# Second expert stage of a two-block model: sixteen weight slots on the chip, the expert sum kept in the residual, the silu written in place

## The reference, cut to what matters

```python
x  = ln_affine(ALPHA * x + (1 + m[2]) * hyena(h), ln_g[0], ln_b[0])
hl = modulate(x, m[3], m[4])
# 16 experts; each one takes the 64 tokens with the highest affinity for it:
#   y[tokens] += affinity * ((silu(hl[tokens] @ w1) * (hl[tokens] @ w3)) @ w2)
x  = ln_affine(ALPHA * x + (1 + m[5]) * y, ln_g[1], ln_b[1])
```

## Time and profile before

| | us |
|---|---|
| median of 3 runs | 2311.09 |
| lowest, highest | 2307.94, 2311.12 |
| the profiled execution's own time | 2322.09 |
| its span, first to last instruction | 2320.1 |

### The profile page before, as it was taken

The page is one execution under the profiler, slowest core; times in us unless marked ns, Lnnn a source line. Parts: engine busy times, 40 slices in busy tenths (PEclk is TensorE's granted clock), DMA queues, the critical chain, the costliest instruction groups (busy, mean ns, idle before and its releaser), DMA issues.

```text
span 2320.1 us, 25225 instructions
## 1 busy us (share of the span) xinstructions
PE 1948.7 (84%) x9836; PEld 1138.1 (49%) x9836; DVE 755.2 (33%) x1283; ACT 539.6 (23%) x910; POOL 273.7 (12%) x187
## 2 busy tenths in 40 slices
PE   7888978785898983899988599888888888888886
PEld 5776876563454552687976233232333333333332
DVE  5546333333332325565873601011010101010103
ACT  4765544321212124431133300000000000000002
POOL 1750700002222222000420000000000000000000
PEclk9897989897999996899998699999999999999998
DMA  5641461037999955122223189999999999999993
GB/s 195 236 181 67 188 260 62 0 154 268 391 402 419 402 222 219 73 91 91 73 73 138 81 350 413 422 413 421 413 422 414 421 414 422 414 421 415 420 416 151
DMA packets 127896, 640.87 MB, mean 276 GB/s; under 512 B 13675, under 2 KB 30443, under 8 KB 72908
## 3 DMA queue, kind: packets, MB, share of 16 engines
q1 hardware_dynamic: 112956, 606.78, 65.0%
q0 software_dynamic: 4304, 16.52, 1.9%
q10 hardware_dynamic: 10560, 16.52, 1.9%
HBM read 608.83 MB, written 30.93 MB: 276 GB/s over the span
## 4 chain that ended last, share of the span: by engine, by line
PE 46%; DMA 30%; DVE 9%; ACT 6%; POOL 6%; issue 2%; SPq 1%; ACTq 0%; DVEq 0%; POOLq 0%
PE psum L818 45%; DMA ring<-in_w 28%; DVE arena L1843 2%; POOL arena L779 2%; PE psum L816 2%; ACT arena L1502 1%; DVE weights_low L1843 1%; ACT arena L1475 1%; DVE arena_low L1843 1%; DVE arena L1851 1%; POOL arena L775 1%; DMA ring<-in_stream 1%; POOL arena L776 1%; ACT arena L1509 1%; DVE arena L1847 1%
## 5 line engine op out<-in xcount | busy, mean ns | idle before, releaser
L818 PE MATMUL psum<-ring,arena 128*64 128x512 f32 x3816 | 855.6, 596 | 122.4 <-DMA ring<-in_w 111.7
L818 PEld LDWEIGHTS psum<-ring,arena 128*64 128x64 f32 x3816 | 297.7, 137 | 653.0 <-issue 636.9
L1475 ACT ACTIVATE arena<-psum 128x512 f32<-128x512 f32 (+3 forms) x231 | 119.8, 544 | 1051.7 <-PE psum L818 992.4
L1843 DVE TENSOR_TENSOR arena<-psum,arena 128x512 f32<-128x512 f32 (+1 forms) x112 | 73.2, 653 | 662.4 <-PE psum L818 555.2
L818 PE MATMUL psum<-arena_low,weights_high 128*128 128x512 f32 (+1 forms) x704 | 255.6, 382 | 7.1 <-DVE weights_low L1843 7.1
L818 PE MATMUL psum<-features_high_part,weights_high 128*128 128x512 f32 x576 | 232.8, 404 | 33.5 <-DVE weights_low L1843 15.1
L818 PE MATMUL psum<-features_high_part,weights_low 128*128 128x512 f32 x576 | 229.6, 399 | 0.0
L818 PE MATMUL psum<-arena 128*128 128x512 f32 (+4 forms) x514 | 189.2, 525 | 11.4 <-ACT arena L1475 9.7
L1843 DVE TENSOR_TENSOR weights_low<-ring,weights_high 128x2048 fp32r<-128x2048 f32 x46 | 110.2, 2400 | 153.4 <-ACT weights_high L1493 144.9
L816 PE MATMUL psum<-ident,arena 128*128 128x128 f32 (+2 forms) x556 | 79.9, 290 | 87.4 <-DVE arena L1847 31.9
L818 PEld LDWEIGHTS psum<-arena_low,weights_high 128*128 128x128 f32 x704 | 134.0, 197 | 30.7 <-DVE weights_low L1843 7.3
(11 more groups left out here) (241 smaller groups left out, 1639.3 us busy)
## 6 DMA issues: line engine op xcount, KB each, us to landing
ring<-in_w SPq DMA_DIRECT2D x384, 1024.0 KB, 20.2
ring<-in_moe SPq DMA_DIRECT2D x93, 1024.0 KB, 10.3
ring<-in_stream SPq DMA_DIRECT2D x54, 1024.0 KB, 6.8
arena<-in_stream SPq DMA_DIRECT2D x16, 1024.0 KB, 4.9
in_spectra<-ring ACTq DMA_DIRECT2D x8, 1024.0 KB, 23.9
ring<-in_spectra SPq DMA_DIRECT2D x8, 1024.0 KB, 5.9
x_places<-scratch POOLq DMA_DIRECT2D x1, 7936.0 KB, 36.8
arena<-x_places SPq DMA_DIRECT2D x15, 512.0 KB, 12.0
```

What stands on the lines that cost most here:

```text
L818: ins_ = pe.matmul(o, lhs, rhs, start=start, stop=stop)
L1475: bk.emptied.inc(act.activation(dst, o, func, **more))
L1843: return dve.tensor_tensor(dst, a, b, op)
```

## The change

- The stage has 16 slots. Twelve are the ring as before. Four lie in the arena: two in region 1 (where `y2` was), one in the upper half of region 2, one in the upper half of region 3 (where `silu2` was). Slot 12 is loaded only after the last output of the second layer normalisation, since region 1 is read until then.
- `y2` and its memset are gone. Each scatter product is multiplied by (1 + m[5]) and added to `x`, which has been multiplied by ALPHA before the loop. The eight steps behind the loop are gone, and the last layer normalisation reads `x`; PE's first means wait for DVE's emptying of the scatter banks instead of `s_res`.
- The silu is written into `hid2`, and DVE multiplies in place.
- `y_sel`, `onehot`, `onehot_g` move to region 4, `scat` to `scratch`.

```diff
--- before.py
+++ after.py
@@ -34,7 +34,8 @@
 COLS = UNIT // KD
 RING = 5
 RING1 = 9
-RING2 = 12
+RING2 = 16
+WHOLE = 12
 ALPHA = 2.0 ** 0.25
 LN_EPS = 1e-5
 MOD_EPS = 1e-6
@@ -249,7 +250,7 @@
 
 
 
-        ring = under("ring", [P, RING2, UNIT])
+        ring = under("ring", [P, WHOLE, UNIT])
         w_low = [part(f"weights_low{r}", [P, UNIT]) for r in range(RING + 1)]
         w_high = [part(f"weights_high{r}", [P, UNIT]) for r in range(HIGH)]
         f_high = part("features_high_part", [P, KD, S])
@@ -400,15 +401,16 @@
         window_const = nc.inline_tensor(filter_windows(), "filter_windows").ap()
 
         h_tok = region(5, 0, ST, D)
-        y2 = region(1)
         x_sel = region(2, 0, 1, D)
         x_sel_t = region(2, 1024, KD, P)
-        y_sel = region(2, 2048, 1, D)
-        onehot = region(2, 3072, ST, P)
-        onehot_g = region(2, 3584, ST, P)
-        hid2, silu2 = region(3, 0, 1, FF), region(3, 2048, 1, FF)
+        y_sel = region(4, 2048, 1, D)
+        onehot = region(4, 3072, ST, P)
+        onehot_g = region(4, 3584, ST, P)
+        hid2 = region(3, 0, 1, FF)
         hid2_t = region(4, 0, FF // P, P)
-        scat = arena[:, 4, 2048:2560]
+        scat = scratch[:, 0, :]
+        moe2_slot = [ring[:, n, :] for n in range(WHOLE)] + [arena[:, 1, UNIT * b:UNIT * b + UNIT] for b in range(2)]
+        moe2_slot += [arena[:, 2, UNIT:2 * UNIT], arena[:, 3, UNIT:2 * UNIT]]
         aff_t = arena[0:NE, 4, 2560:3072]
         work_t = arena[0:NE, 4, 3072:3584]
         mask_t = arena[0:NE, 4, 3584:4096]
@@ -542,7 +544,7 @@
                 slot_ = turn[0] % slots
                 if used.i is not None or turn[0] >= slots:
                     sp.wait_ge(s_used, used.at(1 - slots))
-                dst = ring[:, slot_, :]
+                dst = moe2_slot[slot_] if arrived is s_arrived2 else ring[:, slot_, :]
                 if dst_shape is not None:
                     dst = dst_shape(dst)
                 sp.dma_start(dst, src).then_inc(arrived[slot_], 16)
@@ -699,6 +701,8 @@
                 for name in ("w1", "w3"):
                     for k in range(KD):
                         for e in range(2):
+                            if name == "w1" and 2 * k + e == WHOLE:
+                                sp.wait_ge(s_lno, 6 * KD)
                             load(ins[name][2 * i + e, k])
                 for k in range(KD):
                     for e in range(2):
@@ -835,7 +839,7 @@
                 pe.wait_ge(arrived[slot_], v)
                 turn[0] += 1
                 unit_no.n += 1
-                return ring[:, slot_, :]
+                return moe2_slot[slot_] if arrived is s_arrived2 else ring[:, slot_, :]
 
             def used():
                 owed.append(s_used)
@@ -1453,7 +1457,7 @@
                     mm(o, y_sel[:, 0, P * n:P * n + P], scat, True, True, bk_d)
                 assert not owed
                 leave(entry)
-            layer_norm(region(2), region(3), lambda k: pe.wait_ge(s_res, KD + k + 1))
+            layer_norm(x, region(3), summed)
 
 
         @block.scalar
@@ -1795,7 +1799,7 @@
                 bk.filled.enter(i, 12)
                 bk.emptied.enter(i, 12)
                 for n in range(4):
-                    empty(take(), silu2[:, 0, 512 * n:512 * n + 512], ACT.Silu)
+                    empty(take(), hid2[:, 0, 512 * n:512 * n + 512], ACT.Silu)
                 gathered()
                 for n in range(2):
                     o = take()
@@ -2473,8 +2477,6 @@
                     ins_.then_inc(s_aff, 1)
                 else:
                     do(ins_)
-            dve.wait_ge(s_lno, 6 * KD)
-            do(dve.memset(y2, 0.0))
 
             dve.wait_ge(s_ea, note["aff_t"])
             do(dve.tensor_copy(work_t, aff_t))
@@ -2511,6 +2513,7 @@
                             ins_.then_inc(s_ohg if gated else s_oh, 1)
 
             one_hot(0, False)
+            dve.wait_ge(s_lno, 6 * KD)
             do(ts(x, x, ALPHA, ALU.mult))
             after()
             with dve.Fori(0, NE // 2) as i:
@@ -2523,20 +2526,16 @@
                 for n in range(4):
                     o = take()
                     dve.wait_ge(s_ea, 12 * i + note["moe2_a"] + n + 1)
-                    done(tt(hid2[:, 0, 512 * n:512 * n + 512], o, silu2[:, 0, 512 * n:512 * n + 512], ALU.mult))
+                    done(tt(hid2[:, 0, 512 * n:512 * n + 512], o, hid2[:, 0, 512 * n:512 * n + 512], ALU.mult))
                 for n in range(4):
                     o = take()
                     done(dve.tensor_copy(hid2_t[:, 4 * n:4 * n + 4, :], o.rearrange("p (k n) -> p k n", k=4)))
                 for n in range(KD):
-                    done(tt(y2[:, n, :], take(), y2[:, n, :], ALU.add))
+                    done(stt(x[:, n, :], take(), modp[:, 40 + n:41 + n], x[:, n, :], ALU.mult, ALU.add))
                 bk.filled.leave(NE // 2)
                 bk.emptied.leave(NE // 2)
             after_bank()
-            for n in range(KD):
-                stt(region(2)[:, n, :], y2[:, n, :], modp[:, 40 + n:41 + n], x[:, n, :], ALU.mult, ALU.add)\
-                    .then_inc(s_res, 1)
-            dve.wait_ge(s_res, 2 * KD)
-            layer_norm(region(2), region(2))
+            layer_norm(x, region(2))
 
 
 # ---- launch: one core; the host only lays arrays out ----
```

## The result

| | before | after |
|---|---|---|
| runs in the comparison | 8 | 8 |
| median, us | 2315.51 | 2303.78 |
| lowest, highest | 2307.94, 2319.65 | 2299.38, 2309.32 |
| profiled execution, its span | 2322.09, 2320.1 | 2309.32, 2307.3 |

The ratio is 0.9945, 95% interval 0.9926 to 0.9963: 12.7 us faster (0.0055 x 2315.5). The direction was right. The time lies outside the range: 2294.9 was forecast, 2290.5 to 2301.5, and 16.2 us were to be gained. Of the eight runs before, three are those that the prediction had (2307.94 to 2311.12); the five later ones lie at 2315.03 to 2319.65, median 2316.55. The profiled executions differ by 12.8 us. Where these lie, and where the missing 3.4 us are, is the question of the rest.

A forecast was written before the change was run, and what follows sets the result against it. The prediction took expert-weight transfers to set the pace once PE starts the stage. It summed 9.95 (prefetch) + 1.0 (memset) + 5.3 (end) = 16.2 us, giving a median of 2294.9 us, range 2290.5 to 2301.5.

The forecast's parts named there:

- Four more units ahead of the stream: Expert stage's weight stream: four w1 units loaded before PE starts leave 368 units instead of 372, saving 9.95 us.
- The end: Behind the last scatter: means unpaced by DVE, copy 4.9 us earlier; first `along_rows` 0.9 less, second 0.5 more; 5.3 us saved.
- The memset: Routing ahead of the stage: without it DVE's affinity copy, then PE's start and the stream, come 1.0 us earlier.
- main case: All terms hold: 16.2 us saved, median 2294.9, with its bounds 2292.0 to 2300.3; chance 0.73.
- the base of the sum: Whole kernel: gain summed on the profiled 2322.09 us, then carried to the median of the runs, 2311.09.
- How the numbers follow: Part of the prediction giving chances of main case and rivals, and the range 2290.5 to 2301.5 us.
- A: Routing ahead of the stage: the burst of four loads delays the routing chain 4 us, result 2299; chance 0.08.
- B: Ahead of the stream: nothing of the prefetch arrives, 6.3 us are left, result 2304.8; chance 0.06.
- C: Expert stream: the deeper ring also quickens it, 368 units at 2.487 us, 8.5 us more, 2286.4; chance 0.06.
- D: Whole stage: arena use and more outstanding loads slow the stream 24.7 us, 8.4 us slower overall, 2319.5; chance 0.05.

The follow-up runs named there:

- first pair: Profiled executions of the first comparison, unaltered changed kernel against the kernel before: spans 2307.3 and 2320.1 us.
- three later ones: Changed kernel unaltered, timed again beside the kernel before on three occasions: ratios 0.9917, 0.9928 and 0.9930; medians 2301.74, 2303.32 and 2299.93 us.
- fourth changed profile: Profile of the unaltered changed kernel from its third repeat against the kernel before; that repeat measured 2299.93 us, ratio 0.9930.
- first changed profile: Profile of the unaltered changed kernel from the first comparison with the kernel before: 2309.32 us, span 2307.3; comparison ratio 0.9945.

## Why the prediction was wrong

**The mechanisms and their prices held.** Four more units ahead of the stream: 9.95 us forecast, 10.24 in the first pair, 10.2 when undone. Their wait was satisfied, as argued, with the queue idle. The turns kept their length. The Trainium skill ("DMA: Bandwidth & Descriptors", Specifications) lists 358 GB/s as the limit of HBM for each core, half of 716 GB/s for a pair; the estimate by that was 11.7 us. This kernel runs on one core, its stream moved 418 GB/s, and the measured 10.2 us sides with the rows. The end: 5.3 forecast, 5.2 measured, 5.4 when undone, and its two halves as taken: 1.96 us for eight steps of means (0.245 a step, forecast 0.23), 1.16 us for the first `along_rows`, 2.08 for the second. The memset: the copy came 1.0 us earlier, with ACT late next. One slip in the bounds: 5.6, 0.9 and 0.3 are 6.8, not 6.9, which moves one end of the main case by 0.1 us.

**A term that was too large.** The memset's 1.0 us was carried whole to PE's start; 0.6 arrived. What was wrong is "Everything behind it (top-k, one-hots, gather) moves with it": the gather's duration is not fixed, 9.0 to 9.9 us by when the granted clock rises. It is a small miss, of 0.4 us.

**The step that put the time outside the range** is the base of the sum: "the median of the runs is 2311.09, 11.0 us lower, and I carry the difference over to it unscaled", and with it, in "How the numbers follow", "The three runs lie 3.2 us apart, so I add 1 us or so." I took the median of three runs for the kernel's time, and their distance for the scatter. The same kernel's median came out at 2315.5, 2321.0, 2318.9, 2317.7 and 2315.9 in larger samples, its single runs between 2307.9 and 2323.0. The three runs were on the fast side by some 7 us; against the five later runs of the same comparison (2316.55) it is 5.5. The measured 2303.78 lies 8.9 us above the forecast: 5.5 us are this base, 3.4 us the smaller gain of this one comparison (12.8 us against the five later runs). On 2317.8, the mean of the five medians, the forecast gain gives 2301.6, and the changed kernel's four medians are 2303.8, 2301.7, 2303.3 and 2299.9. That the profiled execution lay 11 us above the median was in front of me: an execution of this kernel can be 11 us off, so a median of three can be several. Widening alone would not quite have done: plus or minus 8 us around 2294.9 ends at 2302.9. The base itself was too low. Why just these three runs were fast stays open: neither their chip nor their granted clock is on record.

**The first comparison's gain** of 12.7 us has 16.2 within its interval (8.6 to 17.1 us); three later ones gave 19.3, 16.7 and 16.2. In the first pair of profiles the difference is 3.25 us, 3.2 of them in the first 39 us of the program, in instructions that are the same in both. That the sum of 16.2 us agrees with the mean of four comparisons to the tenth is luck beside their spread of 12.7 to 19.3; that its terms agree with the cuts of the profiles is not.

**Rivals.** A (the burst delays the routing chain): the cut to the copy is 1.0 us shorter, as it would be without any delay, while the DMA share beside it was 0.92; out. Two packets of instruction fetches, 0.02 MB together, fell into the same 11 us. Instruction fetches that the Trainium skill ("Runtime: NRT & Kernel Launch", Instruction fetch mechanics) calls mostly hidden stayed hidden here, by the same cut. B: out by the stretch of 932.4 us. C: out by the run with twelve units early, whose ring is as deep and whose stretch is 942.63. D: out by the turns.

## What to carry to other kernels

A stream that saturates the DMA engines, as this one did at a share of 1.02, ended earlier only by what was on chip before it started, at one transfer time a unit (or by its start itself); slots that were free during the idle stretch ahead of it were worth that much, and a deeper ring during the stream nothing. Where a tail of element-wise steps can be folded into work that another engine paces, it costs nothing there, and here the engine that follows worked without a pause and kept 2.4 GHz for one step more. A forecast of an absolute time needs the scatter of the baseline's medians, not the spread of three runs; cutting two profiles at a few events separates the change from it, if TensorE's steps between the events are seen to have had the same clock.

## What the runs showed of the hardware that was not expected

The granted clock of TensorE rises at different points in executions of one program. Between the two profiles of the kernel before, that is 3.6 us at 190 us and 3.0 us at 1090 us of the span. In the routing the router's products took 8.3 to 10.0 us and the gather 9.0 to 9.9 us, for the same reason: a fast router (fourth changed profile) has 1.2 GHz for about its first 3 us, a slow one (first changed profile) for about 6.

A clock at 2.4 GHz was lost across waits of 1.9 and 1.7 us with 0.4 us of work between them, and kept when both were filled, in one profile each.

With sixteen slots SP's issue itself became slow. Instructions that write the ring and the arena, issue durations (min/median/max ns), before and then after:

```profile
L548 SPq DMA_DIRECT2D ring<-in_w x384: 328/333/4202, 1255.8 to 2263.4; - x192
```

```profile
L550 SPq DMA_DIRECT2D arena<-in_w x96: 332/2012/3446, 1298.7 to 2254.6; - x96
```

A median issue of 0.33 us before, 2.0 us after, with the median landing at 20.2 us before and 24.0 and 25.9 us after. It costs nothing here: with sixteen slots but only twelve units early the issue into the arena is as slow (2.01 us), and the stretch is the 942.6 us of the kernel before. What limits the issue was not tried. The profile's chain of waits after the change passes through SP several times for 2.5 to 3.1 us, though the turn is as long as before: a share in that chain is not a price.
